# Joining each token's two expert rows in TensorE instead of adding them on VectorE and GpSimd

## The reference, cut to what matters

```
x = x + gate2 * hier_moe(h)        # a token's two expert rows are summed here
y = rms_norm(x, final_norm_w)      # x * rsqrt(mean(x*x) + eps) * final_norm_w
```

## Time and profile before

| what | us |
|---|---|
| three runs, sorted | 1421.61, 1426.04, 1431.02 |
| the profiled execution | 1422.58 |
| its span | 1420.9 |
| TensorE busy | 1294.3 |
| VectorE busy | 739.2 |
| GpSimd busy | 283.1 |

### The profile page before, as it was taken

How to read it: one execution, slowest core, us unless ns; L and a number is a source line. 1 busy time by engine, 2 the same in 40 slices (tenths; PEclk the granted TensorE clock), 3 DMA queues, 4 the chain that set the end, 5 groups by cost and what they waited for, 6 DMA issues and landing times. The chain is left out here.

```text
span 1420.9 us, 19388 instructions
## 1 busy us (share of the span) xinstructions
PE 1294.3 (91%) x6905; PEld 926.0 (65%) x6905; DVE 739.2 (52%) x1429; ACT 262.1 (18%) x562; POOL 283.1 (20%) x399
## 2 busy tenths in 40 slices
PE   5999999999999999999989988999999799887763
PEld 2787667788778777767777766888878533222222
DVE  1534588898877767010126558775666522111125
ACT  2201211222223334010122222400002300000001
POOL 0214334333333433122200002000002301111001
PEclk9899999999999999999999998999999799999995
DMA  9452243333331333655541112412244699999944
GB/s 361 165 113 86 71 150 119 119 101 107 119 119 60 119 119 112 228 176 186 192 173 45 31 30 110 147 60 89 88 175 186 231 420 419 420 419 419 420 172 186
DMA packets 65283, 250.88 MB, mean 177 GB/s; under 512 B 9803, under 2 KB 19435, under 8 KB 51979
## 3 DMA queue, kind: packets, MB, share of 16 engines
q1 hardware_dynamic: 48546, 213.34, 40.0%
q0 software_dynamic: 10112, 20.47, 4.3%
q10 hardware_dynamic: 6536, 15.90, 3.9%
HBM read 234.47 MB, written 22.91 MB: 181 GB/s over the span
## 5 line engine op out<-in xcount | busy, mean ns | idle before, releaser
L362 PE MATMUL psum<-arena 128*128 128x272 f32 x2408 | 568.5, 394 | 7.9 <-DVE arena L1303 5.4
L362 PEld LDWEIGHTS psum<-arena 128*128 128x128 f32 x2408 | 452.7, 189 | 119.2 <-issue 23.7
L384 POOL TENSOR_TENSOR arena<-arena 128x512 f32<-128x512 f32 x96 | 126.7, 1319 | 209.6 <-DMA arena<-in_weights 162.1
L2800 PE MATMUL psum<-arena 128*64 128x512 f32 x512 | 119.0, 610 | 22.1 <-DMA arena<-in_w_gu 19.7
L1467 PE MATMUL psum<-arena 128*128 128x272 f32 x512 | 123.1, 398 | 0.0
L1467 PEld LDWEIGHTS psum<-arena 128*128 128x128 f32 x512 | 96.4, 191 | 25.7 <-DVE arena L1593 3.6
L2800 PEld LDWEIGHTS psum<-arena 128*64 128x64 f32 x512 | 35.9, 138 | 94.6 <-issue 71.6
L2822 PE MATMUL psum<-arena 128*64 128x512 f32 x256 | 65.3, 655 | 17.4 <-issue 15.0
L1593 DVE TENSOR_TENSOR arena<-arena,psum 128x272 f32<-128x272 f32 x16 | 7.0, 440 | 133.4 <-ACT arena L1544 133.4
L2874 DVE TENSOR_TENSOR arena<-arena,psum 128x256 f32<-128x256 f32 x16 | 6.8, 422 | 131.9 <-ACT arena L2865 131.9
L1787 PE MATMUL psum<-arena 128*128 128x272 f32 x256 | 64.1, 404 | 3.0 <-PEq L206 3.0
(11 more groups left out here) (382 smaller groups left out, 1508.4 us busy)
## 6 DMA issues: line engine op xcount, KB each, us to landing
arena<-in_weights SPq DMA_DIRECT2D x153, 512.0 KB, 4.6
arena<-in_w_gu SPq DMA_DIRECT2D x32, 2048.0 KB, 33.7
arena<-in_w_down SPq DMA_DIRECT2D x16, 2048.0 KB, 35.3
arena<-in_weights ACTq DMA_DIRECT2D x16, 512.0 KB, 4.2
arena<-in_pages_k POOLq DMA_DIRECT2D x40, 128.0 KB, 3.5
arena<-in_x SPq DMA_DIRECT2D x2, 2176.0 KB, 13.2
arena<-in_pages_v SPq DMA_DIRECT2D x32, 128.0 KB, 3.2
arena<-in_pages_v POOLq DMA_DIRECT2D x32, 128.0 KB, 3.4
```

What stands on the lines that cost most here:

```text
L362: mm = pe.matmul(out, lhsT=w[:, c * P:c * P + P], rhs=x[:, c, :], start=(c == 0 and not added), stop=(c == 3), skip_group_check=added or more)
L384: link(dve.tensor_tensor(sums[:, k], a, b, op))
L2800: mm = pe.matmul(psum[CAP * e:CAP * e + CAP, 2 + k, :].rearrange("p (o f) -> p o f", o=2), lhsT=xgT[:, k, lo:lo + CAP], rhs=wv[:, e, c4], ...
```

## The change

The row additions on VectorE and GpSimd go, with their two semaphores. TensorE waits for a block's load itself. In place of each transpose it does two plain products by the identity that accumulate in the same place of PSUM, one of the token's first row and one of its second. For the last block (3) it signals after every two chunks, which is one bank, and the second half's residual waits bank by bank.

```diff
-            BY_POOL = (1, 3)
...
             @block.tensor
             def _(pe):
-                for n, i in enumerate(ORDER):
+                for i in ORDER:
                     m = P if i < 4 else NEW
-                    if i in BY_POOL:
-                        pe.wait_ge(s_yc2, BY_POOL.index(i) + 1)
-                    else:
-                        pe.wait_ge(s_yc, [k for k in ORDER if k not in BY_POOL].index(i) + 1)
+                    pe.wait_ge(s_yrs[i], 16)
                     if i == 4:
                         pe.wait_ge(s_yres, DC)
                     for c in range(DC):
-                        mm = pe.transpose(turned(c, i), yr[0:m, i, c * P:c * P + P], const("ident", m)[:, 0:m])
-                    mm.then_inc(s_yt, 1)
+                        for w in range(2):
+                            mm = pe.matmul(turned(c, i), lhsT=yr[0:m, i, w * D + c * P:w * D + c * P + P],
+                                           rhs=const("ident", m)[:, 0:m], start=(w == 0), stop=(w == 1))
+                        if i == ORDER[-1] and c % 2:
+                            mm.then_inc(s_yt, 1)
+                    if i != ORDER[-1]:
+                        mm.then_inc(s_yt, 1)
...
-            @block.gpsimd
-            def _(pool):
-                for i in BY_POOL:
-                    pool.wait_ge(s_yrs[i], 16)
-                    a, b = yr[:, i, 0:D], yr[:, i, D:2 * D]
-                    pool.tensor_tensor(a, a, b, ALU.add).then_inc(s_yc2, 1)
-
             @block.vector
             def _(dve):
...
-                def rows_added(i):
-                    m = P if i < 4 else NEW
-                    dve.wait_ge(s_yrs[i], 16)
-                    a, b = yr[0:m, i, 0:D], yr[0:m, i, D:2 * D]
-                    dve.tensor_tensor(a, a, b, ALU.add).then_inc(s_yc, 1)
-
                 def residual(half):
 
-                    dve.wait_ge(s_yt, 2 if half == 0 else NR)
                     for c in range(DC):
+                        dve.wait_ge(s_yt, 2 if half == 0 else NR + c // 2)
...
-                rows_added(0)
-                rows_added(4)
                 residual(0)
-                rows_added(2)
                 dve.wait_ge(s_yt, 3)
```

More of the change, by code:

```diff
@@ L2953, in _ @@
                     weights(r + 2)
-            s_yc, s_yc2, s_yt, s_yres, s_sq13, s_ss13, s_std13, s_y13, s_r13, s_rs13 = (sem(n) for n in (
-                "y_rows_added", "y_rows_added2", "y_rows_turned", "y_residual", "squares3",
+            s_yt, s_yres, s_sq13, s_ss13, s_std13, s_y13, s_r13, s_rs13 = (sem(n) for n in (
+                "y_rows_turned", "y_residual", "squares3",
                 "square_sums3", "std3", "y_ready", "rstd3_ready", "rstd3_spread"))
```

## The result

The changed kernel took 1436.16 us in the median of 8 runs (1430.94 to 1439.11), against 1423.44 us for the kernel before, which by then also had 8 (1420.51 to 1431.02). The ratio is 1.0074, 95% interval 1.0052 to 1.0095: slower by 7 to 14 us, most likely 10.5 (the two medians themselves lie 12.7 apart). My forecast was 1 us faster, and 1436.16 lies outside the range I gave.

The account below looks back on a forecast made before the run. TensorE was busy 91% of the span, but only the 37 us tail is edited. The second residual starts at 1405.3 against 1406.26, so -1.0 us: 1426.0 - 1.0 = 1425.0 us, range 1419.5 to 1431.5.

Parts of the forecast that it names:

- the price of a plain product: TensorE's tail products: 0.112 us each at the full clock, 0.22 at the half, about a transpose's price.
- the bound of 0.217 for the half clock: Lower bound on a plain product's half-clock price, from the product with 9 columns: (1.88 - 0.36)/7.
- the other bound, 0.44: Upper bound at the half clock: twice a transpose's price there, if weight loads and products did not overlap.
- The rule I dismissed: Skill's four passes for true FP32: estimated 0.21 us a product at the full clock, 0.43 at the half.
- Rival 4: Tail: a plain product costs twice the charge, 0.44 and 0.224 us; +6.5 us, or +16 to +19 at half clock; chance 0.04.
- the forecast's clock: Tail: full from about 1393.6 in block 1, lost in the pause ahead of block 4, back after 4.5 us of work.
- The clock at block 1 and in the pause: Full for block 1, turned at 1395.5 (-2.3 us); taken as fallen after the 3.3 us idle ahead of block 4.
- The other rule: Skill's claim that transposes do not engage the full clock; the prediction said the trace disagrees, with the return at 1405.7.
- the idle stretch: TensorE's wait ahead of block 4, 3.3 us idle, after which the full clock was taken as lost.
- block 1's landing: Block 1's load lands at 1393.4, so neither block 0's removed addition nor its slower products matter.
- GpSimd's absence: First residual: stays at 3.23 us, as the second with GpSimd idle takes 3.23 too, so nothing is gained.
- the signals by bank: Second residual: VectorE starts after 36 of 48 products; the other 12 (1.35 us at full clock) run beside it.

Follow-up runs that it names:

- block 4 last: Changed kernel with blocks in order 0, 1, 2, 3, 4, TensorE waiting ahead of block 2 only for the first residual instruction: tail 32.5 us, ratio 1.0038 to before.
- One product: Changed kernel with one plain product for each 128 features instead of two, the token's second row left out: tail 27.3 us, ratio 0.9973 to before.
- one transpose: Changed kernel with one transpose in place of the two products, the token's second row left out: tail 23.3 us, ratio 0.9977 to before.
- joined transposes: Changed kernel with its two products in transpose mode, the second accumulating onto the first: tail 25.8 us, ratio 0.9988 to the kernel before.
- without signals by bank: Changed kernel with the second residual waiting for all of block 3 instead of bank by bank: tail 40.5 us, ratio 1.0064 to the kernel before.
- TensorE kept at work: Changed kernel with 15 extra identity products into unread bank 4, between block 1 and the wait ahead of block 4: tail 32.7 us, ratio 1.0028 to before.

## Why the prediction was wrong, point by point

**The step that failed is the price of a plain product.** I wrote "38 in 4.40 us, (4.40 - 0.27)/37 = 0.112". The 38 are records and not products. Line 665 stands in loops that make 5 blocks x 2 heads x 8 chunks = 80 products. The trace of the kernel before has 160 records of it:

```profile
L665 PE MATMUL psum<-arena x160: 270/273/297, 94.3 to 112.1; 128*128 128x128 f32 x128, 128*32 128x128 f32 x32
```

So a float32 product is two weight loads and two matmuls, 0.22 us at the full clock and 0.43 at the half, while a transpose of the same size is one record, 0.117 and 0.22. The same slip is in "568.5/2408", in line 1877's 32 records for 16 products, and in line 512's eight records, which are four products: so the bound of 0.217 for the half clock was half a product's price too, and the other bound, 0.44, was the right number, for a reason (loads and products not overlapping) that no run tested. With 36 products behind the first residual I had charged for 36 records where there were 72. I compared two rates per record and called them prices per instruction of the program. Both the loop's count and the lengths of the weight loads (146 ns in the mean at the transposes of line 2780, 192 at line 665) were in reach.

**The rule I dismissed was right.** That the trace "disagrees with it by a factor of two" came of that slip alone. The Trainium skill's four passes for true FP32 (FP8 and Floating Point Precision, TensorE Precision Notes) make 0.21 us at the full clock, by an estimate from 128 columns; the 96 records in 11.07 us with block 4 last make 0.23. The trace agrees, to about a tenth. For 272 columns the same estimate is 0.45, and two records of the 0.236 I had worked out make 0.47. Another page of the Trainium skill speaks against the edit too (Perfetto Trace Analysis, Transposes): a logical transpose should be a transpose and not a standard matmul. One product against one transpose, 3.77 and 1.97 us for a block, agrees with it.

**Rival 4 is what happened**, given 0.04. It put +6.5 us with the forecast's clock and +16 to +19 with the half clock throughout; the tail has +8.7 and the runs some 10.5. Its first half was too dark by 1.0: in this execution the clock returned at 1391.7, 3.2 us after the first product, so 64 records ended at 1397.4 and cost nothing against the kernel before (13.9 us to the first residual, where it was 13.8). That is in part luck: in the four other kernels with the same 64 records it took 3.6 to 6.2 us, and the first stretch 14.2 to 15.5, which may be why the timed runs lost more than this tail. Its second half was too light, by 2.9 (13.7 from residual to residual, where it was 16.6): I let the clock return 4.5 us after the third batch began, and it took until 1412.2, 11.4 us after.

**The clock at block 1 and in the pause: right in kind.** With prices as I had them (joined transposes) block 1 ran at full, the third batch began at full, fell within its first microsecond, and took 7.97 us; I had 4.5 at half and the rest at full, which is 4.5 + 28 x 0.112 = 7.6. The other rule stays contradicted. The Trainium skill (TensorE: Matmul & The Clock Gate, Part 4: PE-mode transpose) has transposes not engage the full clock, and in the kernel with joined transposes TensorE did nothing else from 1396.89 on, in the kernel before nothing else from 1390.38 on. Its row for the microsecond from 1400 has the clock at 0.88, so it rose at 1400.2, within block 0:

```profile
1400.00:1401.00 1.00, 0.47 (x3) 0.16 (x1) 0.00 (x0) 0.00 (x0) 0.00 (x0) 0.88 0.93 287
```

The cause of the fall was incomplete. I named the idle stretch alone. It is one cause, since without signals by bank the clock fell inside it; but with TensorE kept at work it fell too, behind block 4's thin products, and with block 4 last it stayed up until they were done.

**The rest held.** The additions' removal and block 1's landing were as written; GpSimd's absence left the residual at 3.23 us; the signals by bank, put alone into the kernel before, gave 0.9 us in the middle stretch, though only 0.4 of the 0.7 to 1.3 that was expected of the tail; with joined transposes the tail shrank by 1.1 us where I had said 1.0. In the changed kernel the residual did not run through in 3.23 but took 3.56, since four products (eight records, 0.90 us) outlast two of its instructions (0.81). The chance of 0.97 for no change beyond 1% stands: 1.0074. The range's upper end, 1431.5, left rival 4 out; with its +6.5 in place of +2.6 the same sum gives 1435.5, so even then 1436.16 lay outside. The sum had a slip as well: two thirds of the runs' spread are 2.9 us below the median and 3.3 above, and I had put 3.3 below and 3.0 above.

## What to carry to other kernels

Before a count of records is used as a price, divide it by the count that the loop in the program makes: the two differ by two for float32 products and not for float32 transposes. Where TensorE has to transpose and add, let the transposes accumulate; they cost half of products by the identity, and that alone turned a loss of 8.7 us of tail into a gain of 1.1. And where a bank is waited for, wait for the instructions that read that bank and no more: with it and the joined transposes the middle of the tail went from 8.4 us to 5.7.

## What the runs showed of the hardware that I had not expected

A transpose of float32 accumulates onto an earlier one in PSUM at its usual price: 16 in 1.97 us at the full clock, whether the second overwrites or adds. And TensorE's granted clock can fall while it is never idle: at 1410.6 with its last pause before 1393.35, 1.1 us behind 32 records of 32 rows and 32 columns; the same records at the end of the work left 7.3 us of wide ones at 2.4 GHz.
